# A two-layer hybrid decoder step on one core: the order of the first layer's DMA queue and of its first softmax denominators

## The reference

```python
q, k, v, gate = swa_project(rmsnorm(x), w_in, q_norm, k_norm)        # 16 heads of 64, 4 key/value heads
logits = einsum('bnqkgd,bnskd->bnkgqs', q, k) * HEAD_DIM**-0.5 + bias  # window of 128 plus 16 meta keys
probs  = softmax(concatenate([logits, sink]))[..., :-1]              # a learned sink for each head
o      = einsum('bnkgqs,bnskd->bnqkgd', probs, v)
x      = x + (o * silu(gate)) @ w_out                                # samples: the same over their caches
```

## Time and profile before

| | |
|---|---|
| median of 3 runs | 2241.38 us |
| the profiled execution | 2245.53 us |
| its span, first to last instruction | 2243.7 us |
| PE busy | 2137.0 us (95%) |
| DVE busy | 1052.4 us (47%) |
| ACT busy | 769.2 us (34%) |
| POOL busy | 486.2 us (22%) |
| mean granted TensorE clock | 0.969 of full |

### The profile page before, as it was taken

How to read it: one execution, slowest core, us unless ns; L and a number is a source line. 1 busy time by engine, 2 the same in 40 slices (tenths; PEclk the granted TensorE clock), 3 DMA queues, 4 the chain that set the end, 5 groups by cost and what they waited for, 6 DMA issues and landing times. The chain is left out here.

```text
span 2243.7 us, 32879 instructions
## 1 busy us (share of the span) xinstructions
PE 2137.0 (95%) x13089; PEld 1872.0 (83%) x13089; DVE 1052.4 (47%) x1843; ACT 769.2 (34%) x1609; POOL 486.2 (22%) x479
## 2 busy tenths in 40 slices
PE   4999979999999999999999999994999999999999
PEld 4999977777899999998999899983669669669668
DVE  6322246855645313540354035405773773773772
ACT  3114657852333322332233223322431431431431
POOL 3000005642321000100010001001450450450540
PEclk8999988999999999999999999995999999999999
DMA  6641122003532232223222322226775575585673
GB/s 215 78 92 40 38 53 77 1 8 120 173 90 87 83 131 67 87 93 128 60 87 97 126 61 84 97 83 174 230 246 162 172 246 159 176 251 151 191 247 90
DMA packets 321886, 272.20 MB, mean 121 GB/s; under 512 B 57958, under 2 KB 268454, under 8 KB 321651
## 3 DMA queue, kind: packets, MB, share of 16 engines
q1 hardware_dynamic: 307854, 221.58, 33.2%
q10 hardware_dynamic: 13880, 48.52, 6.6%
HBM read 168.89 MB, written 102.11 MB: 121 GB/s over the span
## 5 line engine op out<-in xcount | busy, mean ns | idle before, releaser
L369 ACT ACTIVATE sb_whi<-sb_wraw 128x1024 fp32r<-128x1024 f32 x108 | 114.2, 1058 | 454.6 <-PE ps L390 375.9
L374 DVE TENSOR_TENSOR sb_wlo<-sb_wraw,sb_whi 128x1024 fp32r<-128x1024 f32 x108 | 141.8, 1313 | 270.4 <-ACT sb_whi L369 263.9
L390 PE MATMUL ps<-sb_h1h,sb_whi 128*128 128x358 f32 x1152 | 252.9, 327 | 0.0
L390 PE MATMUL ps<-sb_h1h,sb_wlo 128*128 128x358 f32 x1152 | 252.8, 327 | 0.0
L390 PE MATMUL ps<-sb_h1l,sb_whi 128*128 128x358 f32 x1152 | 251.4, 326 | 0.0
L390 PEld LDWEIGHTS ps<-sb_h1h,sb_whi 128*128 128x128 f32 x1152 | 199.1, 189 | 2.0 <-issue 1.8
L390 PEld LDWEIGHTS ps<-sb_h1l,sb_whi 128*128 128x128 f32 x1152 | 199.2, 189 | 0.0
L390 PEld LDWEIGHTS ps<-sb_h1h,sb_wlo 128*128 128x128 f32 x1152 | 199.1, 189 | 0.0
L1049 POOL COPY sb_ctail<-sb_xr 128x3 f32<-128x3 f32 x16 | 3.0, 188 | 698.2 <-DVE sb_xr L1182 698.2
L1768 PE MATMUL pm<-sb_cst,sb_qs 128*128 128x512 f32 x256 | 133.0, 602 | 0.0
L390 PE MATMUL ps<-sb_hh,sb_whi 128*128 128x358 f32 x480 | 116.2, 351 | 15.1 <-DVE sb_hl L412 11.9
(11 more groups left out here) (400 smaller groups left out, 4684.5 us busy)
## 6 DMA issues: line engine op xcount, KB each, us to landing
sb_scs<-state_mlstm_c SPq DMA_DIRECT2D x32, 1024.0 KB, 5.7
sample_mlstm_c<-sb_scs SPq DMA_DIRECT2D x32, 1024.0 KB, 5.1
sb_wraw<-mlstm_w_in SPq DMA_DIRECT2D x48, 512.0 KB, 3.9
sb_wraw<-swa_w_in SPq DMA_DIRECT2D x20, 512.0 KB, 3.8
scratch_ga<-sb_st ACTq DMA_DIRECT2D x16, 537.0 KB, 2.9
scratch_gb<-sb_st ACTq DMA_DIRECT2D x16, 537.0 KB, 4.3
scratch_v<-sb_st ACTq DMA_DIRECT2D x16, 537.0 KB, 2.9
scratch_q<-sb_st ACTq DMA_DIRECT2D x16, 537.0 KB, 2.9
```

The source lines that it names most:

```text
L369: act.activation(whi[q][:, :], wraw[q][:, :], ACT.Copy).then_inc(sem("w_hi"), 1)
L374: dve.tensor_tensor(wlo[q][:, :], wraw[q][:, :], whi[q][:, :].bitcast(F32), ALU.subtract)\
L390: last = pe.matmul(ps[s][:, g, 0:GRP], w[:, kk, c * P:(c + 1) * P], x[:, kk, g * GRP:(g + 1) * GRP], start=(kk == 0 and i == 0), stop=(kk ...
```

## The change

Four edits, all in the first layer; no instruction is added or removed on any engine:

- the sinks' load goes behind the first two bias DMAs (those of key/value head 0);
- the 8 small `brow` loads go from ahead of the bias to behind the samples' bias (`biasS`), 52 DMAs further down;
- in the output product's list, `x1_load(1, 0)` now comes directly behind `x1_load(0, 0)`, and `samp_loads(2)` behind it. Every later sample's load also stands one tile later: sample b comes behind `x1_load(b-1)`, where it came behind `x1_load(b-2)`;
- DVE's denominator of unit 0 goes from behind the softmax step of unit 2 to behind that of unit 1.

```diff
-            sp.dma_start(sinkb[:, :], dram(a["swa_sinks"], 0, [[0, P], [1, NH]])).then_inc(sem("sinkb_in"), 16)
-            for r in range(0, P, 32):
-                for f in range(2):
-                    sp.dma_start(brow[r + MH - MH * f:r + 2 * MH - MH * f, :],
-                                 dram(a["mlstm_b_gates"], MH * f, [[1, MH], [1, 1]])).then_inc(sem("brow_in"), 16)
             for kv in range(KVH):
                 bias_load(kv, slice(2 * P, KEYS), RBAND + P - 1, RROW)
                 bias_load(kv, slice(P, 2 * P), 2 * P - 1, RROW)
+                if kv == 0:
+                    sp.dma_start(sinkb[:, :], dram(a["swa_sinks"], 0, [[0, P], [1, NH]])).then_inc(sem("sinkb_in"), 16)
...
+            for r in range(0, P, 32):
+                for f in range(2):
+                    sp.dma_start(brow[r + MH - MH * f:r + 2 * MH - MH * f, :],
+                                 dram(a["mlstm_b_gates"], MH * f, [[1, MH], [1, 1]])).then_inc(sem("brow_in"), 16)
             turned_all(sp)
...
             for j in range(KT):
                 x1_load(sp, j, 0)
-                if j + 2 < DECB:
-                    samp_loads(sp, Idx(j + 2))
+                if 0 < j < DECB - 1:
+                    samp_loads(sp, Idx(j + 1))
...
             for s in range(3):
                 dve.wait_ge(sem(f"bias_in{s}"), 32)
                 att_softmax_dve(dve, Idx(s))
-            att_den(dve, Idx(0))
+                if s == 1:
+                    att_den(dve, Idx(0))
```

## The result

The changed kernel takes 2236.17 us (median of 7 runs, 2230.72 to 2238.69), the kernel before on the same chip 2246.60 (7 runs, 2240.53 to 2247.92); ratio 0.9961, 95% interval 0.9949 to 0.9974, so 5.8 to 11.5 us faster (the ratio is taken with its interval from the single runs and says 8.8 us; the two medians are 10.4 us apart). A second set of runs gave 2235.34 us (5 runs) and 0.9952 (0.9940 to 0.9964). Faster, as forecast, but the time lies 6.2 us over the predicted 2230.0 and 1.0 us outside the range.

What follows compares the result with a forecast made beforehand. PE, busy almost throughout, was taken to set the pace, with time to gain only where it idles or runs at low clock. 5.1 + 8.3 - 2.0 = 11.4 us off the 2241.4 median gave 2230.0 us, range 2225.5 to 2235.2.

Steps and rivals of the forecast that it cites:

- Part 1: Start of the attention: bias ahead of sinks and `brow` ends DVE's bias wait earlier; gain 0.3 us, ends -0.9 and +0.4.
- at most 0.36: Start of the attention: upper limit in us of the earlier bias's gain, since DVE then waits for PE's scores.
- Part 2: Start of the attention: denominator one softmax step earlier starts PE's transposes 5.1 us sooner, bias gain included; ends 2.6 and 8.1.
- a clock fixed in time: Start of the attention: if the clock returned at 351 us regardless of the work, 2.5 us of gain would be lost.
- Part 3: Output product: weight and residual ahead of the sample's loads close PE's hole; 4.9 + 2.7 + 0.7 = 8.3 us gross.
- No hole, no low clock behind it: Output product, values of sample 1 to next key transposes: full clock makes 10.62 us into 7.91, gaining 2.7 us.
- The 0.7 for the late residual: Output product: later residuals come earlier, so the 11.58 us key-transpose period after tile 3's late residual shrinks by 0.7 us.
- The price, 2.0: Output product: loads of samples 6 and 7, now behind a store, make PE wait; 2.0 us lost, ends 0 and 3.8.
- Rival 1: Attention start and output product: clock fixed in time and loads at their upper end leave 7.1 us, 2234.3; chance 0.18.
- Rival 2: One of the holes at attention start and output product stays open: gain 6.3 or 5.1 us, 2235.1 or 2236; chance 0.13.
- Rival 3: Start of the attention: the clock returns early, 3 us more, so 14.4 us gained, 2227; chance 0.08.
- Rival 4: Output product: late loads of samples 6 and 7 starve PE and the clock falls again, slower at 2243.2; chance 0.03.

Runs made afterwards that it cites:

- part 3 alone: The kernel before with only weight and residual ahead of sample 2's loads and every later sample's loads one tile later; 2240.51 us, ratio 0.9974.
- the changed kernel without part 1: The changed kernel with sinks and `brow` loads put back ahead of the bias, the other edits kept; 2235.47 us, ratio 0.9947 to the kernel before.
- the four executions with part 3 as it is: Profiles of the changed kernel (2236.17 and 2235.34 us), part 3 alone (2240.51) and the changed kernel without part 1 (2235.47), without later changes to the loads' or query copies' order.
- the changed kernel's first profile: Profiled execution of the changed kernel with all four edits against the kernel before; it took 2238.52 us with a span of 2236.7 us.
- the third profile of the kernel before: The kernel before, unchanged, run and profiled a third time; 2244.80 us, ratio 1.0001.
- part 2 alone: The kernel before with only DVE's denominator of unit 0 moved behind the softmax step of unit 1; 2241.87 us, ratio 0.9981.

## Why the prediction was right and wrong

**Part 1, +0.3.** Right in size, for partly other reasons. L507 began 11.27 to 11.83 us behind the head's zero in the seven executions without part 1 (mean 11.42) and 10.68 to 11.44 in the six with all of it (mean 11.15): 0.27 us earlier. What I missed: "at most 0.36" came from one execution in which PE's scores ended late, at 11.0 us. The bias ended the wait at 11.3 to 11.4 in six of the seven, but the scores ended anywhere from 9.8 to 11.6. And with the bias directly behind the swapped keys, the scores (L494) begin 8.73 instead of 8.14 us behind the zero (means of the same groups), which takes back a good part of what the earlier bias could give. Whether the bias traffic holds back the swapped keys' landing was not tried by itself. The sinks came at 9.59, where I had 9.55 (321.3 less 311.75), and that was luck: the two bias DMAs ahead of them took SP 4.11 us to issue instead of 1.16, so they went out 3.0 us later than reckoned (319.91, 5.57 behind the zero), and then needed 4.0 us instead of 6.95. The time can't tell this part from nothing.

**Part 2, 5.1 with part 1.** Right. L507 to L543 shrank by 4.95 us, and H has a median of 183.5 without the part (five executions) and 178.0 with it (nine): 5.5 us. On the clock the rows' account was the better one. Its return from the low level came 37.6 to 39.6 us behind the zero in four of the five executions without the part and 33.1 to 34.3 in eight of the nine with it: it moved along with the work, and the 2.5 us of a clock fixed in time were lost in none of them. Around this the return scatters: it came at 47.0 with part 3 alone and at 25.7 in the changed kernel without part 1. These two extremes lie about 3.5 us of H to either side, and the second, 8.7 us under the 183.5, is past my upper end of 8.1. Fourteen microseconds from 26.0 us behind the zero, of these two:

```profile
338.25:352.25 14.00, 13.31 (x70) 0.50 0.15 37
```
```profile
338.50:352.50 14.00, 14.00 (x126) 1.00 0.18 42
```

**Part 3, 8.3 gross.** The hole of 4.9 closed: the first values product L808 begins 18.5 us behind the first residual's issue in all nine executions with part 3, 23.2 to 23.7 in the five others. The step of the mechanism that failed is "No hole, no low clock behind it", the term of 2.7. I took L808 to the next key transposes from a neighbouring sample (7.91 us) and did not ask whether DVE's copies for L760, so far hidden beside PE's slow products, would be ready. The stretch takes 8.83 us where the clock stays up and 10.35 where it falls. Before it took 10.62 in the first profile and 10.6 to 11.4 in the five executions without part 3 (mean 11.0); against that mean the term was worth 1.5 on average of the four executions with part 3 as it is. With the copies taken ahead the stretch takes 7.94, the size I had predicted.

The 0.7 for the late residual stands in the period of sample 5, 11.58 us in the earlier trace rows. PE's wait in it that came from tile 3's late residual, by way of DVE, is this one in the kernel before:

```profile
548.21 0.30 PE L827 MATMUL pm<-sb_ident,sb_obS 128*64 128x128 f32 x1 [0.52 <-DVE sb_obS L822]
```

It is in all five executions without part 3 (0.3 to 1.4 us) and in none of the nine with it. The period as a whole did not come back to 10.9 everywhere, since sample 5's loads are waited for in some executions: 11.59 in the changed kernel's first profile, 10.87 in its second. It has a mean of 12.3 us without part 3 and of 11.4 in the four with it as it is: 0.9 gained.

**The price, 2.0.** Measured 0.7 to 1.1 (mean 1.0 in the four) on samples 6 and 7, by the store as reasoned. Sample 5's wait for its loads is no price of part 3: it is 0 to 1.1 us with the part, and 1.27 in the third profile of the kernel before and 1.08 with part 2 alone. In both orders these loads go out only 3.5 us ahead of where PE wants them, and the 3.45 us that I took for the most they need was no such bound: in seven of the 14 executions PE waited for them, until 4.1 to 4.9 us behind their first issue.

**The sum and the base.** O has a mean of 92.8 us in the four executions with part 3 as it is, of 99.1 in the five without: 6.3 us, which is the predicted 8.3 - 2.0. That it fits is luck: measured it is made of 4.9 + 1.5 + 0.9 - 1.0, so the clock's term fell short by 1.2 us, and the price and the late residual made up for it. With 5.5 of H the two stages gained 11.8, where I had 11.4.

The time was missed, all the same, mostly by another step, the last one of the sum: "against this median of 2241.4 the sum gives 2230.0". The base 2241.38, median of three, lay low in a wide scatter. In later sets the kernel before had medians of 2245.78 (35 runs), 2245.58 (11) and 2245.36 (18), and single runs from 2235 to 2256 us. Of the 6.2 us by which the forecast missed, 5.2 are the distance between the base used and the 2246.60 of the comparison. My own sentence said that the profiled execution lay 4.1 us over this median; its 2234.1 was the better number. The remainder is that code without a change gave some back: the ratios say 8.8 and 10.8 us, not 11.8. In the profiles, "rest" is 1.4 us longer on average with part 3 (nine executions, 1648.3 to 1652.5) than without (five, 1647.0 to 1650.6), and the work ahead of the head's zero 2 us longer in most of the later kernels than in the three profiles of before. The low clock goes with both. Half of PE's busy time in the stretches at the low level is 6.2 to 8.4 us ahead of the zero in the three and 8.6 to 11.2 in the others; in "rest" it is 21.3 us with part 3 and 20.3 without, on average, which is 1.1 of the 1.4. Whether that is chance of so few executions stays open.

**The rivals.** Rival 1 (7.1 us) named the right weak places, clock and loads, and the first profile's span (7.0 us shorter) looks like it; the mean over executions does not, and neither of its two terms came as reasoned. Rival 2 fell: both holes closed. Rival 3's early return was seen once (174.81). Rival 4 fell: with part 3 the longest wait at L740 was 1.1 us. The Trainium skill's statement in TensorE: Matmul & The Clock Gate, part 1, that the monitor's window runs freely of the kernel's work, fits what the executions of one kernel show here: the same code meets the fall in one and not in the next (0.74 and 1.00 above). What I drew from it, that the return would not slide along with the work, the runs do not bear out: the scatter lies around a place that does slide.

## What to carry to other kernels

Ahead of an absolute forecast, look at how far the profiled execution and the few timed runs lie apart: here a base of three runs was 4 to 5 us off, more than any term of the sum was missed by. When a hole is closed, go through all engines for work that the hole, or the slow clock behind it, had hidden, not only for the one that ended the hole; the query copies were such a thing, and moving them gave the predicted 7.9 us. A sum that fits does not show that its terms do: two of part 3's four terms were off by 1 us or more, the two misses against each other. A queue order that takes one wait away puts the next one directly behind it: the store could be put behind the loads as well, and then neither waited.

## What the runs showed of the hardware

- **The clock goes either way at a marginal place.** In 14 profiled executions there are four such places: 3 us behind the head's zero it fell in nine and not in five; its return in the head came between 25.7 and 47.0 us behind that zero; at the end of the attention the low stretch cost 1.5 to 1.7 us of PE's time in ten and 2.9 to 3.2 in four; behind the start of the output product, once the hole is closed, it fell in two of nine, which cost 1.5 us. Seven runs of the changed kernel spread over 8 us of 2236, and one pair of profiles tells a gain of 2 us from chance only if the lengths are taken stage by stage.
- **A hole costs more than itself.** The hole of the output product, 4.6 to 5.1 us of idle PE, was followed by the low clock in each of the five executions that had it, and the stretch behind it took 10.6 to 11.4 us, against 7.94 with neither hole nor wait: 2.6 to 3.5 us more.
- **Some small DVE operations beside a POOL operation on 128x716 end only with it.** Every copy of 64x8 (L728) and operation on 128x1 (L816) that began well inside L920 (2.2 to 2.3 us), 42 in the 14 executions, took 1.65 to 1.68 us instead of some 0.16 and ended 0.01 to 0.03 us behind it. It is no rule for all small operations: L836, which reads one of its operands from the matmul accumulator (`pm`), kept its usual 0.15 us in all 224 cases beside L920, as here in the changed kernel, where L920 runs from 553.72 to 555.99. Why the kinds differ was not tried.

```profile
554.32 0.76 DVE L836 TENSOR_TENSOR sb_ogS<-pm,sb_gate 64x8 f32<-64x8 f32 x8
```

- **A sample's five loads are used 3.5 to 4.9 us behind the first one's issue**, with as much as 1.3 us of waiting in one execution of the kernel before and none in the other two; a lead of 3.5 us is no margin.
